# Weight blocks of queries and groups loaded in pairs into a ring of four slots

## The chip, the cores and the metric

The kernel runs on one core of a Trainium2 chip. The metric is the device time of one execution in microseconds (us), the median of several runs. Matrix products run on TensorE (PE), elementwise work on VectorE (DVE), ScalarE (ACT) and GpSimd (POOL); SyncE (SP) issues most transfers between memory and the on-chip buffers. Each engine has a queue of its own, worked through in order; engines wait for each other by semaphores.

## The reference

One layer of a hybrid encoder over 16 meta tokens and 1024 frames of width 2048, all float32, cut to what matters:

```
h    = concat([meta, x])                       # (16 + 1024, 2048)
proj = rmsnorm(h, norm_g) @ w_in               # 2048 -> 4352 columns
pv, pg, q, k, v, ag = split(proj)              # 1024,1024,1024,128,128,1024
pool_out = (trailing_mean(pv, 2|4|8|16) - pv) @ pool_w * pool_scale   # 4 groups of 256
attn_out = softmax([q k^T / 8, sink]) v        # 16 heads of 64, window of 2 chunks of 64 + meta
h = h + concat([silu(pg) * pool_out, silu(ag) * attn_out]) @ w_out
return h[16:]
```

## The kernel before

**Precision by splitting.** Every float32 operand of a big product is split in two fp32r parts. For a block of weights, ACT copies `raw` to `wh` (the high part, `split_high`, line 618), DVE subtracts to get `wl` (the low part, `split_low`, line 966), and PE makes three products: high times high, high times low, low times high (lines 1435, 1436 and 1442).

**Blocks.** The input projection is cut in blocks of 128x512 float32, 256 KB each, laid out by the host in the order of use (`w_in_blocks`). Frames are done in two halves of 512; each half goes through the same 136 blocks: 8 for keys and values, 32 for queries (8 tiles of 4 blocks), and 4 groups of 24 (attention gate, pooled values, pooling gate). In this text blocks are numbered 0 to 271 over both halves in the order of use; in the second half, block 136 + n is block n of the half. The number of a block in its group is called its slot in the program. After them come 112 blocks of the output product, numbered from 272, which the change does not touch.

**Two rings of four.** `raw` has four slots (`RAW = 4`), and so have `wh` and `wl` (`SPLIT = 4`); block n has slot n % 4 in all. The life of block n is:

1. SP waits until block n - 4 has been split by DVE, since that frees the slot of `raw` (`s_wl`, line 399), and issues the load (line 400). Each slot has its own semaphore of landing, `s_raw[slot]`.
2. ACT waits for the landing (line 621) and until PE has finished block n - 4 (`s_blk`, line 624), since that frees the slot of `wh`; then it copies. In ACT's program the split of block n stands three blocks ahead of the products that use it (`LEAD = 3`), among the rest of ACT's work: exponentials, copies of transposed probabilities, tanh of the gates.
3. DVE waits for `wh` and writes `wl` (line 970).
4. PE waits for `wl` and makes the block's 12 or more products; the last one raises `s_blk`.

**The other queues that matter.** In a group, four units of attention are woven between the blocks: PE makes scores, DVE and ACT the softmax, PE transposes the probabilities (line 1605), ACT and DVE split the result (`pt`, `pm`; `p_high`, line 849, and `p_low`, line 1183), and PE multiplies by the values (line 1617). The blocks in the program of each engine at which these stand are fixed by `UNIT_AT`. POOL, beside the sums of pooling, issues 32 transfers of 1 MB (two at each of 16 places) that prepare sums of output weights in memory (`weight_sums`, lines 540 to 558): two places lie in the queries of each half and six at the ends of its first three groups. In the first half's groups 1 to 3, SP also stores finished tiles to memory (`spill`, line 411) after block 6 of the group, and loads frames of the next half (`next_frames`, line 418) after block 14.

Of the kernel before, what the change touches and what calls it, by code (L numbers as in the profile page):

```python
# [21 lines left out]
HALVES = SEQ // HALF  # L22
# [18 lines left out]
ONE = 1  # L41

BLK = 512
TILE_BLKS = 4
RAW = 4
SPLIT = 4
LEAD = 3
KV_BLKS = 2 * TILE_BLKS
Q_BLKS = PAIRS * TILE_BLKS
G_BLKS = 6 * TILE_BLKS  # L50
IN_BLKS = KV_BLKS + Q_BLKS + GROUPS * G_BLKS
# [20 lines left out]
OUT_AT = HALVES * IN_BLKS  # L72
# [18 lines left out]
def hymba_layer(nc, xcat, norm_g, w_in, w_out, pool_w, vecs, consts, out):  # L91
# [6 lines left out]
    with ctx:  # L98
        def sb(name, shape, dt=f32):
            return ctx.enter_context(nc.sbuf_tensor(name, shape, dt))  # L100

        def sem(name):
            return ctx.enter_context(nc.semaphore(name))
# [5 lines left out]
        raw = sb("raw", [P, RAW, BLK])  # L109
# [135 lines left out]
        s_xc = sem("s_xc")  # L245
        s_sp = sem("s_sp")
        s_raw = [sem(f"s_raw{i}") for i in range(RAW)]
        s_pw = sem("s_pw")
        s_init = sem("s_init")
        s_gq = sem("s_gq")  # L250
# [3 lines left out]
        s_wl = sem("s_wl")  # L254
# [140 lines left out]
        def _(sp):  # L395
            def load_block(n, slot, src, free=True):

                if free:
                    sp.wait_ge(s_wl, ONE + n - RAW + 1)
                sp.dma_start(raw[:, slot, :], src).then_inc(s_raw[slot], 16)  # L400

            def first_frames(i):
                k0, k1 = FIRST_LOADS[i]
                lo, hi = k0 % 4 * P, (k1 - 1) % 4 * P + P
                sp.dma_start(mixed[:, k0 // 4:KT:4, lo:hi],
                             xcat[META:META + HALF, k0 * P:k1 * P].rearrange("(r p) c -> p r c", p=P)).then_inc(s_xf[i], 16)
# [4 lines left out]
            def spill(q):  # L411

                sp.wait_ge(s_me, ONE + 2 * (q + 1))
                sp.wait_ge(s_oe, ONE + UNITS * (q + 1))
                for t in (2 * q, HK + 2 * q):
                    sp.dma_start(mx0[t:t + 2, :, :].rearrange("k p c -> p k c"), mixed[:, t:t + 2, :]).then_inc(s_sp, 16)

            def next_frames(q):

                sp.wait_ge(s_sp, 32 * (q + 1))  # L420
                if q:
                    sp.wait_ge(s_xc, 32 * q)
                for i in range(2):
                    t, f = HK * i + 2 * q, META + HALF + 2 * P * i
                    sp.dma_start(mixed[:, t:t + 2, :],
                                 xcat[f:f + 2 * P, q * BLK:(q + 1) * BLK].rearrange("(r p) c -> p r c", p=P)).then_inc(s_xc, 16)

            sp.dma_start(cst[:, 0:P], consts[:, 0:P]).then_inc(s_id, 16)
            sp.dma_start(x_meta, xcat[0:META, :]).then_inc(s_xmeta, 16)
            first_frames(0)  # L430
            first_frames(1)
            first_block(1, free=False)
            first_frames(2)
            first_block(2, free=False)
            first_block(3, free=False)
# [4 lines left out]
            for h in range(HALVES):  # L440
                h0 = h * IN_BLKS
                for n in range(RAW if h == 0 else 0, KV_BLKS):
                    if h and n == KV_BLKS - 1:
                        spill(GROUPS - 1)
                    load_block(h0 + n, n % RAW, w_in[TILE_BLKS * (n % 2) + n // 2, :, :])
                if h:
                    next_frames(GROUPS - 1)
                with sp.Fori(0, PAIRS) as j:
                    for b in range(TILE_BLKS):
                        n = KV_BLKS + j * TILE_BLKS + b  # L450
                        load_block(h0 + n, b % RAW, w_in[n, :, :])

                def group(g):
                    sp.wait_ge(s_pwl, ONE + h * GROUPS + g)
                    sp.dma_start(pw_raw.rearrange("p (a c) -> p a c", a=2),
                                 pool_w[g, :, :].rearrange("(a p) c -> p a c", p=P)).then_inc(s_pw, 16)
                    for b in range(G_BLKS):
                        n = KV_BLKS + Q_BLKS + g * G_BLKS + b
                        load_block(h0 + n, b % RAW, w_in[n, :, :])
                        if h == 0 and g and b == 6:  # L460
                            spill(g - 1)
                        if h == 0 and g and b == 14:
                            next_frames(g - 1)

                if h == 0:
                    for g in range(GROUPS):
                        group(g)
                else:
                    with sp.Fori(0, GROUPS) as g:
                        group(g)  # L470
# [5 lines left out]
            for n in range(OUT_BLKS):  # L476
                p, s = divmod(n, PASS)
# [6 lines left out]
                src = {P1: w_out[top, one], P2: w_out[bottom, one], Q3: w_out[bottom, two]}.get(j)  # L484
                load_block(OUT_AT + n, n % RAW, wsum[kind, p, top, :] if src is None else src)

                if p == 0 and s in A1_AT:
                    i = A1_AT.index(s)
# [125 lines left out]
        def _(act):  # L614
            def copy(dst, src):
                return nc.scalar.activation(dst, src, ACT.Copy)  # L616

            def split_high(n4, off):

                slot = off % RAW  # L620
                act.wait_ge(s_raw[slot], 16 * (n4 + off // RAW + 1))
                if not (isinstance(n4, int) and n4 == 0 and off < SPLIT):

                    act.wait_ge(s_blk, ONE + n4 * RAW + (off - SPLIT + 1))
                copy(wh[:, slot, :], raw[:, slot, :]).then_inc(s_wh, 1)
# [31 lines left out]
            nc.scalar.activation(junk[:, 0:1], kT[:, 0:1], ACT.Sqrt).then_inc(s_table, 1)  # L657
            act.wait_ge(s_table, 1)
            split_high(0, 0)


# [4 lines left out]
            for h in range(HALVES):  # L666
                h4 = h * IN_BLKS // RAW

                for k in range(2 * h, KT):
                    x_high(h, k)  # L670
                    for off in FIRST_SPLITS[h].get(k, ()):
                        split_high(h4, off)
                    for r in FIRST_STATS.get(k, ()) if h == 0 else ():
                        if r == 0:
                            act.wait_ge(s_cst, 16)
                            for i in range(len(FIRST_LOADS)):
                                act.wait_ge(s_xf[i], 16)
                        first_stats(0, r)
                    if h and k in (5, 7, 9, 11):
                        next_stats(2, (k - 5) // 2)  # L680
                    elif h and k >= 14:
                        next_stats(3, k - 14)
# [7 lines left out]
                for s in range(5, KV_BLKS):  # L690
                    split_high(h4, s + LEAD)
                    if s < 7:
                        if h == 0:
                            first_stats(h, s - 3)
                        else:
                            next_stats(3, s - 3)
# [255 lines left out]
            for n in range(OUT_BLKS):  # L952
                p, s = divmod(n, PASS)
# [832 lines left out]
```

## Time and profile before

| | |
|---|---|
| median of 3 runs | 1179.48 us (1178.87 to 1179.82) |
| the profiled execution's own time | 1178.72 us |
| its span, first to last instruction | 1176.6 us |
| PE busy | 1166.1 us |
| DVE busy | 889.7 us |
| ACT busy | 616.1 us |
| weight loads of 256 KB from `w_in_blocks` | 272, 2.7 us from issue to landing in the median |

The profiled execution is one run; its span leaves out 2.1 us that its device time holds before and after. Busy time of an engine is time in which it worked on an instruction. An engine below 100% is either ahead of others and waiting for them, or is waited for; which of the two, only the waits tell.

### The profile page before, as it was taken

The numbers are of one execution on the slowest core, as the hardware profiler recorded it, in microseconds if no ns is written. First come the engines' busy times: TensorE is split into PE (matmuls) and PEld (weight loads), VectorE is DVE, ScalarE is ACT, GpSimd is POOL, SyncE is SP. The second block draws the span as 40 slices with busy tenths as digits, with TensorE's granted clock in tenths as the row PEclk, the third lists the DMA queues.
The fourth block names the chain that finished last, engine by engine and source line by source line (L and its number), as shares of the span: only waits on it lengthen the run. The fifth ranks groups of instructions, "written<-read, shape, count | busy, mean of one in ns | idle before, by whom it ended". The sixth has DMA issues, their size and how long they took to land.

```text
span 1176.6 us, 17280 instructions
## 1 busy us (share of the span) xinstructions
PE 1166.1 (99%) x5882; PEld 991.8 (84%) x5882; DVE 889.7 (76%) x1545; ACT 616.1 (52%) x1400; POOL 115.5 (10%) x133
## 2 busy tenths in 40 slices
PE   7999999999999999999999999999999999999998
PEld 7888898898898988888888888888888888888887
DVE  4678778787786885678788786987977977656676
ACT  5743366554665655643565655655544544444442
POOL 0000011020040220000011030220400000100001
PEclk9999999999999999999999999999999999999999
DMA  7354339455486333445357372392346544553443
GB/s 242 92 162 156 95 99 218 132 189 184 132 177 179 118 90 108 134 138 171 94 129 179 92 242 76 97 226 81 88 137 223 167 136 134 185 176 123 142 145 134
DMA packets 85486, 171.26 MB, mean 146 GB/s; under 512 B 8464, under 2 KB 11792, under 8 KB 85264
## 3 DMA queue, kind: packets, MB, share of 16 engines
q1 hardware_dynamic: 72000, 129.08, 35.3%
q0 software_dynamic: 13120, 40.90, 14.1%
q8 instruction: 44, 0.72, 0.3%
q14 instruction: 34, 0.28, 0.1%
q10 hardware_dynamic: 288, 0.28, 0.1%
HBM read 157.64 MB, written 46.14 MB: 173 GB/s over the span
## 4 chain that ended last, share of the span: by engine, by line
PE 99%; DMA 0%; DVE 0%; ACT 0%; issue 0%; SPq 0%; DVEq 0%; ACTq 0%
PE R L1435 18%; PE R L1436 18%; PE R L1442 18%; PE R L1725 3%; PE R L1723 3%; PE R L1724 3%; PE OP L1725 2%; PE S L1725 2%; PE OP L1723 2%; PE S L1723 2%; PE OP L1724 2%; PE S L1724 2%; PE S L1593 1%; PE OP L1617 1%; PE OP L1442 1%; PE OP L1435 1%
## 5 line engine op out<-in xcount | busy, mean ns | idle before, releaser
L964 DVE TENSOR_TENSOR wl<-raw,wh 128x512 fp32r<-128x512 f32 x384 | 283.4, 740 | 192.9 <-ACT wh L616 190.6
L616 ACT ACTIVATE wh<-raw 128x512 fp32r<-128x512 f32 x384 | 240.8, 629 | 351.0 <-PE OP L1725 165.9
L1435 PE MATMUL R<-act_h,wh 128*128 128x512 f32 (+5 forms) x1056 | 380.6, 365 | 0.0
L1436 PE MATMUL R<-act_l,wh 128*128 128x512 f32 (+5 forms) x1056 | 378.5, 364 | 0.0
L1442 PE MATMUL R<-act_h,wl 128*128 128x512 f32 (+5 forms) x1048 | 362.2, 365 | 0.0
L1436 PEld LDWEIGHTS R<-act_l,wh 128*128 128x128 f32 x1056 | 198.6, 188 | 28.6
L1435 PEld LDWEIGHTS R<-act_h,wh 128*128 128x128 f32 x1056 | 198.3, 188 | 28.7
L1442 PEld LDWEIGHTS R<-act_h,wl 128*128 128x128 f32 x1048 | 188.3, 188 | 32.1
L1725 PE MATMUL R<-wh,mix_l 128*128 128x512 f32 x168 | 65.4, 389 | 0.0
L1723 PE MATMUL R<-wh,mix_h 128*128 128x512 f32 x168 | 65.4, 389 | 0.0
L1724 PE MATMUL R<-wl,mix_h 128*128 128x512 f32 x168 | 65.4, 389 | 0.0
L870 ACT ACTIVATE row_buf<-scr 128x512 f32<-128x512 f32 x32 | 20.2, 632 | 79.5 <-DVE scr L1212 79.5
L1154 DVE TENSOR_REDUCE scr<-S 128x288 f32<-128x576 f32 x56 | 42.3, 756 | 25.3 <-PE S L1593 24.5
L1084 DVE RECIPROCAL scr<-scr 128x512 f32<-128x512 f32 x16 | 53.6, 3347 | 0.0
L844 ACT ACTIVATE scr<-scr,nmax 128x144 f32<-128x144 f32 x128 | 51.2, 403 | 3.4 <-DVE nmax L1162 3.3
L586 POOL TENSOR_TENSOR scr<-scr 128x513 f32<-128x513 f32 (+6 forms) x40 | 50.3, 1257 | 3.1
L578 POOL TENSOR_TENSOR scr<-scr,row_buf 128x512 f32<-128x512 f32 (+4 forms) x16 | 20.9, 1306 | 268.3 <-ACT scr L616 257.9
L1725 PE MATMUL OP<-wh,mix_l 128*128 128x512 f32 x112 | 43.6, 389 | 0.0
L1724 PE MATMUL OP<-wl,mix_h 128*128 128x512 f32 x112 | 43.6, 389 | 0.0
L1723 PE MATMUL S<-wh,mix_h 128*128 128x512 f32 x112 | 43.6, 389 | 0.0
L1724 PE MATMUL S<-wl,mix_h 128*128 128x512 f32 x112 | 43.6, 389 | 0.0
L1725 PE MATMUL S<-wh,mix_l 128*128 128x512 f32 x112 | 43.6, 389 | 0.0
(252 smaller groups left out, 1957.8 us busy)
## 6 DMA issues: line engine op xcount, KB each, us to landing
raw<-w_in_blocks SPq DMA_DIRECT2D x271, 256.0 KB, 2.7
wsum<-w_out_in POOLq DMA_DIRECT2D x24, 1024.0 KB, 12.1
raw<-wsum SPq DMA_DIRECT2D x64, 256.0 KB, 2.6
raw<-w_out_in SPq DMA_DIRECT2D x48, 256.0 KB, 3.3
c<-xcat SPq DMA_DIRECT2D x32, 256.0 KB, 3.5
out<-c POOLq DMA_DIRECT2D x28, 256.0 KB, 2.9
mixed<-xcat SPq DMA_DIRECT2D x10, 512.0 KB, 5.2
mx<-mixed SPq DMA_DIRECT2D x8, 512.0 KB, 3.5
```

Of the source, the lines that this page charges most:

```text
L586: ins = pool.tensor_tensor(dst[:, lo:COLS], src[:, lo:COLS], src[:, lo - step:COLS - step], ALU.add)
L616: return nc.scalar.activation(dst, src, ACT.Copy)
L844: nc.scalar.activation(prob[:, c, :], prob[:, c, :], ACT.Exp, bias=nmax[:, c:c + 1], accum_out=den[:, c:c + 1]).then_inc(s_ex, 1)
L964: return nc.vector.tensor_tensor(dst, a, b, ALU.subtract)
L1084: nc.vector.reciprocal(q_rs[t % 2], q_rs[t % 2]).then_inc(s_qrs, 1)
L1154: nc.vector.tensor_reduce(to, both, AX.X, ALU.add).then_inc(s_sm, 1)
L1435: mm(o, wh[:, b, w], xh, start=(k == 0), stop=False)
L1436: mm(o, wh[:, b, w], xl, start=False, stop=False)
L1442: last = mm(o, wl[:, b, w], xh, start=False, stop=(k == KT - 1))
L1723: mm(banks[r], mh, wh[:, slot, :], start=(k == 0), stop=False)
L1724: mm(banks[r], mh, wl[:, slot, :], start=False, stop=False)
L1725: last = mm(banks[r], ml, wh[:, slot, :], start=False, stop=(k == HK - 1))
```

## The change

The 256 blocks of queries and groups (128 of each half) are loaded two at a time. A pair (n, n + 1) with n even goes with one transfer of 512 KB into two neighbouring slots of `raw`. The number of slots, the splits on ACT and DVE and the products on PE stay as they are. SP now waits before the pair until block n - 3, which held the slot of the second block, has been split; before, block n was loaded as soon as block n - 4 had been split. Each pair of slots has one semaphore of landing, `s_pair`, so ACT's wait for block n ends only when both blocks are there. `landed` gives the semaphore and the count for each block. Keys, values and the output product are still loaded by `load_block`.

```
+        s_pair = [sem(f"s_pair{i}") for i in range(RAW // 2)]
...
+            def load_pair(n, slot, src):
+
+                sp.wait_ge(s_wl, ONE + n + 1 - RAW + 1)
+                sp.dma_start(raw[:, slot:slot + 2, :], src.rearrange("n p c -> p n c")).then_inc(s_pair[slot // 2], 16)
...
-                    for b in range(TILE_BLKS):
+                    for b in range(0, TILE_BLKS, 2):
                         n = KV_BLKS + j * TILE_BLKS + b
-                        load_block(h0 + n, b % RAW, w_in[n, :, :])
+                        load_pair(h0 + n, b % RAW, w_in[bass.ds(n, 2), :, :])
...
-                    for b in range(G_BLKS):
+                    for b in range(0, G_BLKS, 2):
                         n = KV_BLKS + Q_BLKS + g * G_BLKS + b
-                        load_block(h0 + n, b % RAW, w_in[n, :, :])
+                        load_pair(h0 + n, b % RAW, w_in[bass.ds(n, 2), :, :])
                         if h == 0 and g and b == 6:
                             spill(g - 1)
                         if h == 0 and g and b == 14:
...
+            def landed(n):
+
+                kv, rest = KV_BLKS // RAW, (IN_BLKS - KV_BLKS) // RAW
+                if n >= OUT_AT:
+                    return s_raw[n % RAW], 16 * (HALVES * kv + (n - OUT_AT) // RAW + 1)
+                half, b = divmod(n, IN_BLKS)
+                if b < KV_BLKS:
+                    return s_raw[n % RAW], 16 * (half * kv + b // RAW + 1)
+                return s_pair[n % RAW // 2], 16 * (half * rest + (b - KV_BLKS) // RAW + 1)
...
-                act.wait_ge(s_raw[slot], 16 * (n4 + off // RAW + 1))
+                act.wait_ge(*landed(n4 * RAW + off))
```

SP's queue in group 1 of the first half, before (a row is one kind of transfer, with the shape it writes and how many follow each other):

```order
L455 DMA scr<-pool_w_in 128x2x256
L400 DMA raw<-w_in_blocks 128x512 x7
L416 DMA mx<-mixed 128x2x512 x2
L400 DMA raw<-w_in_blocks 128x512 x8
L425 DMA mixed<-xcat 128x2x512 x2
L400 DMA raw<-w_in_blocks 128x512 x9
```

The same group of SP's queue now:

```order
L461 DMA scr<-pool_w_in 128x2x256
L406 DMA raw<-w_in_blocks 128x2x512 x4
L422 DMA mx<-mixed 128x2x512 x2
L406 DMA raw<-w_in_blocks 128x2x512 x4
L431 DMA mixed<-xcat 128x2x512 x2
L406 DMA raw<-w_in_blocks 128x2x512 x4
```

24 loads became 12 of twice the size; the stores of `spill` now stand behind the loads of 8 blocks instead of 7, and the loads of frames behind 16 instead of 15.

## Rows read from the trace of the kernel before

**Rows 1.** The page, parts 1, 2 and 4: busy time, granted clock, ending chain.

```profile
span 1176.6 us, 17280 instructions
...
PE 1166.1 (99%) x5882; PEld 991.8 (84%) x5882; DVE 889.7 (76%) x1545; ACT 616.1 (52%) x1400; POOL 115.5 (10%) x133
...
PEclk9999999999999999999999999999999999999999
...
PE 99%; DMA 0%; DVE 0%; ACT 0%; issue 0%; SPq 0%; DVEq 0%; ACTq 0%
```

**Rows 2.** Waits of PE (total us, times, longest us), and busy time by stretch.

```profile
PE R L1453 <- DMA scr<-xcat: 5.7, 1, 5.7
PE R L1495 <- DVE act_l L976: 1.0, 1, 1.0
PE OP L1495 <- DVE act_l L976: 0.2, 1, 0.2
...
480.00:866.00 386.00, 386.00 (x1815) 322.17 (x1814) 309.54 (x554) 210.67 (x517) 48.13 (x44) 1.00 0.49 133
```

**Rows 3.** Waits ahead of ACT's split of weights, by what ended them.

```profile
ACT wh L616 <- PE OP L1725: 165.9, 108, 2.4
ACT wh L616 <- PE R L1442: 160.7, 126, 2.8
...
ACT wh L616 <- DMA raw<-w_in_blocks: 9.2, 5, 3.4
```

**Rows 4.** Transfers by source: count, KB each, median us to landing.

```profile
raw<-w_in_blocks SPq DMA_DIRECT2D x271, 256.0 KB, 2.7
wsum<-w_out_in POOLq DMA_DIRECT2D x24, 1024.0 KB, 12.1
...
mixed<-xcat SPq DMA_DIRECT2D x10, 512.0 KB, 5.2
mx<-mixed SPq DMA_DIRECT2D x8, 512.0 KB, 3.5
```

**Rows 5.** Timeline, quiet: DVE splits block 95, the next load, block 98 on ACT, DVE, PE.

```profile
301.44 0.69 DVE L964 TENSOR_TENSOR wl<-raw,wh 128x512 fp32r<-128x512 f32 x1 [1.61 <-ACT wh L616]
302.16 0.33 SPq L400 DMA_DIRECT2D raw<-w_in_blocks  x1
309.76 0.63 ACT L616 ACTIVATE wh<-raw 128x512 fp32r<-128x512 f32 x1 [0.63 <-PE R L1442]
311.85 0.68 DVE L964 TENSOR_TENSOR wl<-raw,wh 128x512 fp32r<-128x512 f32 x1
318.94 0.28 PE L1435 MATMUL R<-act_h,wh 128*128 128x264 f32 x1
```

**Rows 6.** Timeline: blocks 143 and 146 at the start of the second half.

```profile
468.96 0.68 DVE L964 TENSOR_TENSOR wl<-raw,wh 128x512 fp32r<-128x512 f32 x1
472.05 0.62 ACT L616 ACTIVATE wh<-raw 128x512 fp32r<-128x512 f32 x1
476.02 0.29 ACT L715 ACTIVATE scr<-xsd 128x128 f32<-128x128 f32 x1
478.10 0.27 PE L1528 MATMUL PT<-cst,scr 128*128 128x128 f32 x1
```

**Rows 7.** Timeline: one of POOL's 16 places, at the end of group 2 (first half).

```profile
344.27 2.06 POOL L556 DMA_DIRECT2D wsum<-w_out_in  x2
```

**Rows 8.** The load of block 109, its time to landing, ACT's splits of 108 and 109.

```profile
333.96 0.33 SPq L400 DMA_DIRECT2D raw<-w_in_blocks  x1
DMA to landing us min/median/max: 8.5/8.5/8.5
342.16 0.62 ACT L616 ACTIVATE wh<-raw 128x512 fp32r<-128x512 f32 x1
344.88 0.63 ACT L616 ACTIVATE wh<-raw 128x512 fp32r<-128x512 f32 x1 [2.10 <-PE R L1442]
```

**Rows 9.** Loads of blocks 112 and 113; ACT, DVE and PE behind block 112.

```profile
344.91 0.33 SPq L400 DMA_DIRECT2D raw<-w_in_blocks  x1
DMA to landing us min/median/max: 8.4/8.4/8.4
346.43 0.33 SPq L400 DMA_DIRECT2D raw<-w_in_blocks  x1
DMA to landing us min/median/max: 9.1/9.1/9.1
354.25 0.62 ACT L616 ACTIVATE wh<-raw 128x512 fp32r<-128x512 f32 x1
356.55 1.19 DVE L964 TENSOR_TENSOR pm<-OP,pm 16x128 fp32r<-16x128 f32 x4 [0.34 <-ACT pm L616]
359.56 0.64 PE L1617 MATMUL OP<-pt,v_s 128*128 128x256 f32 x4
```

**Rows 10.** The same in the second half: block 249's load, then the chain behind 248.

```profile
773.35 0.33 SPq L400 DMA_DIRECT2D raw<-w_in_blocks  x1
DMA to landing us min/median/max: 9.4/9.4/9.4
781.47 0.61 ACT L616 ACTIVATE wh<-raw 128x512 fp32r<-128x512 f32 x1
783.77 1.19 DVE L964 TENSOR_TENSOR pm<-OP,pm 16x128 fp32r<-16x128 f32 x4 [0.33 <-ACT pm L616]
786.50 0.64 PE L1617 MATMUL OP<-pt,v_s 128*128 128x256 f32 x4
```

**Rows 11.** Second half, group 0: block 197's load, the chain behind block 196.

```profile
610.16 0.33 SPq L400 DMA_DIRECT2D raw<-w_in_blocks  x1
DMA to landing us min/median/max: 7.4/7.4/7.4
617.17 0.63 ACT L616 ACTIVATE wh<-raw 128x512 fp32r<-128x512 f32 x1
620.72 0.63 ACT L616 ACTIVATE wh<-raw 128x512 fp32r<-128x512 f32 x1 [0.74 <-PE R L1442]
629.06 0.22 DVE L1179 TENSOR_TENSOR pnm<-scr,rden 128x64 f32<-128x64 f32 x1
629.37 0.62 PE L1605 MATMUL PT<-cst,scr 128*128 128x128 f32 x4
```

## The prediction

> **What bounds the kernel now.** I read the page first. TensorE is busy for 1166.1 us of a span of 1176.6 us, its granted clock is full in all 40 slices, and the chain that ended last is TensorE for 99% [rows 1]. So a change can win only what TensorE idles, 10.5 us at most, and it loses whatever idle time it puts into TensorE. Next the waits of TensorE: only three are listed, 5.7, 1.0 and 0.2 us, for the meta tokens' transfer at the very start and for DVE's split of the frames, and none for a weight block. From 480 to 866 us, which is nearly all the part of the second half that the change touches, it is busy for 386.00 of 386.00 us [rows 2]. Last, who waits for loads: ACT's split of weights waits hundreds of microseconds for TensorE to free a slot (165.9 and 160.7 us are the two largest) and only 9.2 us, five times, for a load [rows 3]. Loads run ahead of ACT, ACT ahead of TensorE. There is nothing for a better load to win on the path that sets the end.
>
> **What the change removes.** 128 issues of about 0.33 us on SP and 128 landings. SP issues and then waits for DVE's splits; nobody waits for SP's own 0.33 us. That is worth 0. In the groups of the first half the stores of finished tiles and the loads of frames each slip behind one more block: about one block time, some 3 us, and the frames are wanted a group later. Worth 0.
>
> A 256 KB load takes 2.7 us in the median [rows 4]. The Trainium skill would promise more of larger ones: its page "DMA: Bandwidth & Descriptors", section "Anatomy of one DMA", gives a fixed cost of about 2.0 us a transfer and 436 GB/s beyond it, that is 2.6 us for 256 KB (the trace agrees) and, as an estimate, 3.2 us for 512 KB; its section "Bandwidth" advises batches of 1 MB or more. By that rule 128 fixed costs go away, 256 us of transfer latency in all, and by the trace none of it is on the path.
>
> **What it adds: the even block comes later.** The pair (n, n + 1) is issued when block n + 1 used to be, since both wait until block n - 3 is split. So block n + 1 keeps its issue time, and block n is issued later by what lay between the two. And ACT needs block n first, with both now landing together. The question is how far ahead of ACT the odd block's landing lies. I compared these times for all 128 even blocks; two kinds of stretch differ.
>
> *Quiet stretches.* What a 512 KB load to the chip takes is not in the trace, only two other kinds of 512 KB transfer: 3.5 us for stores of tiles and 5.2 us for loads of frames, which run partly under other traffic [rows 4]. I take 3.5, nearest to the undisturbed 2.7 of half the size, and keep 5.2 for the range. A typical place: block 95 is split by DVE at 302.13 (301.44 + 0.69), the pair (98, 99) is issued at 302.16 and lands at 305.7; ACT splits block 98 at 309.76, 4.1 us later [rows 5]. Over all 128 places the median margin is 3.2 us, in the queries mostly 2 to 3. One quiet place fails, at the second half's start: block 143 is split at 469.64, the pair (146, 147) lands at 469.8 + 3.5 = 473.2, and ACT wants it at 472.05, so ACT is late by 1.1 us. Behind it ACT makes the columns that TensorE transposes; they are done at 476.31 and TensorE takes them at 478.10, a cover of 1.8 us [rows 6]. Cost 0; with 5.2 us, late by 2.8, cost 1.0.
>
> *Contended stretches.* At 16 places POOL issues two transfers of 1 MB, as at 344.27 [rows 7]; they take 12.1 us in the median [rows 4], and beside them a weight load takes 6 to 9 us. Here the pair can't land before the odd block did. It lands later still by what the even block's 256 KB take, if these were through before: in this stretch the landings of queued loads follow each other by about 2.1 us (blocks 112 and 113: 344.91 + 8.4 = 353.3 and 346.43 + 9.1 = 355.5, 2.2 apart [rows 9]). Bounds: 0 and 2.1 us on top of the odd block's landing. I take 0.8, since in most of these pairs the even block was itself still queued when the odd one was issued, so that its bytes are counted already. With 0 on top 14 of the 128 even blocks make ACT wait, 10 us in sum; with 0.8, 23 blocks, 23 us; at the far bounds (2.1, and 5.2 us in quiet) 36 blocks, 62 us. Against the 9.2 us of load waits now [rows 3], ACT's waits for loads should come out at some 25 to 35 us.
>
> **What of that reaches TensorE.** A weight split has its own cover: it stands three blocks ahead of its products. Block 98's `wl` is done at 312.53 and its first product starts at 318.94, a cover of 6.4 us [rows 5]; over all 256 blocks of the change the median is 6.8, and only blocks 8 and 144, which are not late, have less than 3.2. That covers the latenesses above by itself. What is thin is the attention work that stands behind a late split in ACT's queue. The late places, by what follows them:
> - Blocks 108, 110, 244 and their like (fourth-last and second-last of a group, and the whole of the queries): late by 0.3 to 2.9. For 108: the odd block lands at 333.96 + 8.5 = 342.5, ACT wants block 108 at 342.16, late 0.3 to 2.4; but ACT then idles 2.10 us waiting for TensorE before block 109 [rows 8]. Absorbed: 0 (at the far bound some 0.3 to 0.8 each).
> - Block 112: late by 355.5 - 354.25 = 1.2 at least, 2.0 by my value, 3.3 at most. Behind it ACT copies `pt` and `pm`, DVE finishes `pm` at 357.74, and TensorE's value products start at 359.56: a cover of 1.8 us [rows 9]. Cost 0 / 0.2 / 1.5.
> - Block 248: the odd block lands at 773.35 + 9.4 = 782.8, ACT wants 781.47: late 1.3 / 2.1 / 3.4; `pm` is done at 784.96, and the products start at 786.50, a cover of 1.5 [rows 10]. Cost 0 / 0.6 / 1.9. Block 224 is like it, late 0.4 / 1.2 / 2.5 with 1.8 of cover: 0 / 0 / 0.7.
> - Block 196: the odd one lands at 610.16 + 7.4 = 617.6, wanted at 617.17: late 0.4 / 1.2 / 2.5. ACT idles 0.74 us three microseconds later, yet the unit's probabilities are done at 629.28 and their transposes start at 629.37, a cover of only 0.1 us at the end of DVE's queue [rows 11]. Between them DVE has short waits of its own, so I take 0 / 0.3 / 1.0.
> - All others (60, 66, 114, 200, 220 and so on): late by 0 / 0 to 1.0 / up to 2.3 with covers above 1.3: 0 / 0 / 1.0 in sum.
>
> Sum at my values: 0.2 + 0.6 + 0.3 = 1.1 us of new idle time on TensorE. Lowest 0; at the far bounds 1.5 + 1.9 + 0.7 + 1.0 + 1.0 + 1.0 (block 146) = 7.1 us. The instructions of TensorE stay the same, and its clock has no reason to fall with idle times of a microsecond.
>
> The profiled execution took 1178.72 us; with 1.1 it is 1179.8. The median of the runs shown, 1179.48, lies 0.76 above it, so I forecast 1180.6. What this measurement can tell from no change is about 0.2%, 2.4 us: below 1177.1 faster, above 1181.8 slower.
>
> **The rivals.**
> 1. *The ring of four is in effect a ring of two, and ACT's lateness gets through.* The mechanism is one: under POOL's traffic a pair lands 2 us behind the old odd block, ACT's split is late by 2 to 3.4 us, and the copy of probabilities behind it starves the value products at 112, 224, 248 and 196. For it: the 2.2 us between queued landings, and that a stall in the first pair delays DVE's split and with it the next pair. Against: ACT's idle time behind every second late split, and the covers of 1.5 to 1.8. Its price is the far sum, 4 to 7 us: 1183 to 1187. It decides from about 2 us of extra landing time on. This is the rival on the slower side.
> 2. *Nothing reaches TensorE.* The pair lands when the odd block did, every lateness is 1.3 us or less and all is covered: 1179.5. For it: the bytes in the queues are the same. Against: only little; it differs from my forecast by 1.1 us and falls in the same class.
> 3. *It becomes faster,* since fewer transfers leave more room for POOL's sums and for the first loads. TensorE has 6.9 us of waits [rows 2], all before the first pair or for frames; a shorter queue could give back perhaps 0.2 us of them. To be 2.4 us faster, TensorE's own instructions would have to run faster beside fewer transfers, for which no row speaks.
> 4. *The change does not do what it says,* that is the 512 KB transfer is carried out as two loads in a row and takes twice as long, 5.4 us, everywhere. Then 5.2 above is the quiet figure: 0 to 2 us on top, 1181.5.
>
> **How the numbers follow.** My forecast, 0.5 to 2.3 us slower, 0.40; rival 2, 0.30; rival 1, 0.22; rival 4, 0.05, half of it over the bound; rival 3, 0.03. Faster 0.03; slower 0.22 + 0.02 = 0.24; the same 0.73. The range reaches from 1178.8, what the median itself scatters on the low side, to 1184.5, which holds the lower part of rival 1.
>
> **What would show it.** In the changed profile: 128 transfers of 512 KB with a median landing time near 3.5 us (well above 4.5 speaks for rival 4); ACT's waits for these loads of 20 to 35 us in some 20 places, most of them beside POOL's 1 MB transfers; TensorE's waits still short, with the new ones, if any, ahead of the value products (now line 1633) near 360 and 786 us or the transposes near 629 us; weight products (now line 1451) waiting for `wl` nowhere. If TensorE waits for `wl` itself, or its new waits add up to over 2.4 us, I am wrong on the cover; if the span shrinks by more than 2 us, I am wrong on the bound.

## The result, and the profile after

The changed kernel takes 1190.42 us in the median of 4 runs (1190.13 to 1191.1), the one before 1179.65 beside it: 10.8 us slower, a ratio of 1.009 with a 95% interval of 1.0078 to 1.0102. The forecast was 1180.6 with a range up to 1184.5. The profiled execution's own time is 1190.54 us, its span 1188.4 us.

The page's parts 1 and 6 after the change answer to [rows 1] and [rows 4]:

```profile
span 1188.4 us, 16928 instructions
...
PE 1170.3 (98%) x5882; PEld 993.6 (84%) x5882; DVE 888.1 (75%) x1545; ACT 617.1 (52%) x1400; POOL 115.5 (10%) x133
...
raw<-w_in_blocks SPq DMA_DIRECT2D x128, 512.0 KB, 3.7
wsum<-w_out_in POOLq DMA_DIRECT2D x24, 1024.0 KB, 12.2
```

The waits of TensorE after the change, all of them (total us, times, longest us), against [rows 2]; and ACT's waits for loads, against [rows 3]:

```profile
PE R L1469 <- DMA scr<-xcat: 5.4, 1, 5.4
PE PT L1621 <- DVE pnm L1195: 2.0, 2, 1.1
PE OP L1633 <- ACT pm L622: 1.9, 2, 1.1
PE OP L1633 <- DVE pm L980: 1.9, 1, 1.9
PE OP L1574 <- DVE d_l L980: 1.7, 1, 1.7
PE R L1511 <- DVE act_l L992: 1.0, 1, 1.0
PE OP L1633 <- issue: 0.5, 1, 0.5
PE OP L1511 <- DVE act_l L992: 0.2, 1, 0.2
```

```profile
ACT wh L622 <- DMA raw<-w_in_blocks: 33.7, 17, 5.7
```

TensorE has five new kinds of wait, 8.0 us in sum, in seven places, and none is for a weight block. They stand ahead of the transposes of probabilities (L1621), the value products (L1633) and the sums of squares of the queries (L1574). ACT's waits for loads went from 9.2 to 33.7 us.

Where the time went, by the ends of the blocks on TensorE, before against after. Each step is the growth of the difference at one block:

| block at which TensorE falls behind | time in the changed profile, us | step, us |
|---|---|---|
| start to block 32, small steps both ways | up to 118 | 0.5 |
| 33 (queries, first half) | 121 | 2.0 |
| 61 and 63 (end of group 0, first half) | 207, 214 | 1.9 |
| 111 (end of group 2, first half) | 369 | 1.3 |
| 195, 197, 199 (end of group 0, second half) | 633 to 647 | 2.6 |
| 247 (end of group 2, second half) | 802 | 3.7 |
| sum, with small steps between | | 11.8 |

The sum is the growth of the span in the two profiled executions. Between these places nothing is lost. The three other executions of the changed kernel have spans of 1187.1 to 1187.2 us, over 1 us shorter than the profiled one, and the medians differ by 10.8, so not every execution has all of the 11.8 us.

**The place at block 34,** which the prediction had priced at 0. Before, with the times of ACT, DVE and TensorE there:

```profile
110.15 0.63 ACT L616 ACTIVATE wh<-raw 128x512 fp32r<-128x512 f32 x1 [2.09 <-PE R L1442]
...
112.81 0.60 ACT L773 ACTIVATE scr<-R 128x512 f32<-128x512 f32 x1 [1.08 <-PE R L1442]
113.31 0.59 ACT L773 ACTIVATE d_h<-R 128x512 fp32r<-128x512 f32 x1
...
114.48 0.69 DVE L964 TENSOR_TENSOR d_l<-scr,d_h 128x512 fp32r<-128x512 f32 x1
...
115.11 0.39 PE L1442 MATMUL OP<-act_h,wl 128*128 128x512 f32 x1
115.33 0.40 PE L1558 MATMUL OP<-d_h,pw_h 128*128 128x512 f32 x1
```

and after, with the pair's issue and its time to landing in front:

```profile
105.01 0.37 SPq L406 DMA_DIRECT2D raw<-w_in_blocks  x1
...
DMA to landing us min/median/max: 9.2/9.2/9.2
...
114.22 0.63 ACT L622 ACTIVATE wh<-raw 128x512 fp32r<-128x512 f32 x1 [5.68 <-DMA raw<-w_in_blocks]
...
116.32 0.59 ACT L789 ACTIVATE d_h<-R 128x512 fp32r<-128x512 f32 x1
...
116.94 0.69 DVE L980 TENSOR_TENSOR d_l<-scr,d_h 128x512 fp32r<-128x512 f32 x1 [0.36 <-ACT d_h L789]
...
117.69 0.50 PE L1574 MATMUL OP<-d_h,pw_h 128*128 128x512 f32 x1 [1.72 <-DVE d_l L980]
```

The pair lands at 105.01 + 9.2 = 114.2 and ends ACT's idle time of 5.68 us. Before, ACT idled 2.09 us there, for TensorE; so the load makes it 3.6 us late. Behind block 34 in ACT's queue stand the squares of a query tile (`d_h`). The cover on this chain was 1.08 us of idle time on ACT ahead of the squares, 0.58 us between their high part (done at 113.90) and DVE's start on the low part (114.48), and 0.16 us between DVE's end (114.48 + 0.69 = 115.17) and TensorE's start (115.33): 1.8 us in all. The other 1.8 us reach TensorE, which waits 1.72 us.

**The place at block 248,** which answers to [rows 10]. The columns of the last two rows are the stretch, its length, the busy us of PE, PEld, DVE, ACT and POOL with their instructions, the granted clock as a share of full speed, the DMA share and GB/s:

```profile
782.89 0.37 SPq L406 DMA_DIRECT2D raw<-w_in_blocks  x1
...
DMA to landing us min/median/max: 10.2/10.2/10.2
...
793.08 0.63 ACT L622 ACTIVATE wh<-raw 128x512 fp32r<-128x512 f32 x1 [2.46 <-DMA raw<-w_in_blocks]
...
795.39 1.19 DVE L980 TENSOR_TENSOR pm<-OP,pm 16x128 fp32r<-16x128 f32 x4 [0.34 <-ACT pm L622]
...
796.63 0.94 PE L1633 MATMUL OP<-pt,v_s 128*128 128x256 f32 x4 [1.86 <-DVE pm L980]
...
797.00:800.40 3.40, 3.40 (x13) 2.81 (x12) 2.81 (x6) 2.55 (x6) 0.00 (x0) 0.50 0.65 128
800.40:806.00 5.60, 5.60 (x26) 4.59 (x25) 4.77 (x10) 1.16 (x2) 0.00 (x0) 1.00 0.16 60
```

The chain is the one of [rows 10], moved: landing, ACT's split, the copies of `pm`, value products, and the cover of 1.5 us is used up. Then comes what no term held: after the 1.86 us of idle time TensorE runs for 3.4 us at the lower granted clock (1.2 instead of 2.4 GHz), which costs 1.7 us more and explains why this step is 3.7 and not 2. It does not come each time: in the profiles of experiments 3 and 9 this place idles 1.46 and 1.82 us and the clock stays full.

The pair of block 248 was not only slow to land, it was also issued late. It waits for DVE's split of block 245, which in turn came late because block 244 did. Before, the split of block 245, and after, ACT and DVE behind the landing of the pair (244, 245) at 779.8 (the profile puts ACT's wait down to TensorE, but it ends with this landing; so it is missing in the 33.7 us):

```profile
772.48 0.69 DVE L964 TENSOR_TENSOR wl<-raw,wh 128x512 fp32r<-128x512 f32 x1
...
779.84 1.15 ACT L622 ACTIVATE wh<-raw 128x512 fp32r<-128x512 f32 x2 [2.47 <-PE R L1458]
...
780.50 0.69 DVE L980 TENSOR_TENSOR wl<-raw,wh 128x512 fp32r<-128x512 f32 x1 [1.96 <-ACT wh L622]
...
782.02 0.69 DVE L980 TENSOR_TENSOR wl<-raw,wh 128x512 fp32r<-128x512 f32 x1
```

The split of block 245 moved by 9.5 us (772.48 to 782.02) where TensorE was only 8.1 us behind, so the pair of block 248 (issued at 782.89) went 1.4 us late. The same happens to the second late pair at the other ends of groups: 0.7 us at block 112, 1.2 us at 64 and at 200.

### The profile page after: what moved, and what is told of

It reads as the page before. It is cut to its first block, busy times and chain, and to the rows that moved or that the text cites. A ratio compares the mean times of both kernels' runs of the same rounds, so it can differ in the third digit from the quotient of the medians.

```text
span 1188.4 us, 16928 instructions
## 1 busy us (share of the span) xinstructions
PE 1170.3 (98%) x5882; PEld 993.6 (84%) x5882; DVE 888.1 (75%) x1545; ACT 617.1 (52%) x1400; POOL 115.5 (10%) x133
## 4 chain that ended last, share of the span: by engine, by line
PE 88%; DMA 6%; DVE 3%; ACT 1%; issue 1%; SPq 0%; ACTq 0%; DVEq 0%
PE R L1451 15%; PE R L1452 15%; PE R L1458 15%; DMA raw<-w_in_blocks 6%; PE R L1739 3%; PE R L1741 3%; PE R L1740 3%; PE S L1739 2%; PE OP L1739 2%; PE OP L1741 2%; PE S L1741 2%; PE OP L1740 2%; PE S L1740 2%; PE S L1609 1%; PE OP L1458 1%; PE OP L1452 1%
## 5 line engine op out<-in xcount | busy, mean ns | idle before, releaser
L1739 PE MATMUL OP<-wh,mix_h 128*128 128x512 f32 x112 | 43.6, 389 | 0.0
```

The source lines that it names most:

```text
L1739: mm(banks[r], mh, wh[:, slot, :], start=(k == 0), stop=False)
```

## The experiments

Each was timed in runs beside the kernel before; "over before" is the difference of the two medians.

**1. Two singles issued when the pair was issued,** each with its own semaphore (change against the kernel before):

```
-                    sp.wait_ge(s_wl, ONE + n - RAW + 1)
+                    sp.wait_ge(s_wl, ONE + n + ahead - RAW + 1)
...
-                        load_block(h0 + n, b % RAW, w_in[n, :, :])
+                        load_block(h0 + n, b % RAW, w_in[n, :, :], free=b % 2 == 0, ahead=1)
```

> Two single loads of 256 KB, each with its own semaphore, both issued when the pair was issued (the even block waits until block n - 3 is split). Nothing else differs from the kernel before. Theory A, the late issue costs: nearly the whole loss of 10.8 us stays, 8 to 11 us, with ACT waiting 25 us or more for loads. Theory B, the common landing costs (ACT needs the even block and gets it only with the odd one): beside POOL's transfers the even block lands 1 to 2 us ahead of the odd one, every lateness shrinks by that, and the loss falls to 0 to 4 us. My guess is 4 us, a part from each.

Measured: 1181.59 us, 1.8 over before, ratio 1.0015 (1.0005 to 1.0024). Its ACT waits 16.8 us for loads, and TensorE has one new wait of 0.8 us before the sums of squares and two short ones before the value products. With a semaphore for each block, the late issue costs about a sixth of the loss. At block 248, the loads of both blocks and then ACT:

```profile
775.90 0.33 SPq L400 DMA_DIRECT2D raw<-w_in_blocks  x1
DMA to landing us min/median/max: 9.0/9.0/9.0
776.43 0.33 SPq L400 DMA_DIRECT2D raw<-w_in_blocks  x1
DMA to landing us min/median/max: 10.6/10.6/10.6
...
784.93 0.63 ACT L616 ACTIVATE wh<-raw 128x512 fp32r<-128x512 f32 x1 [0.95 <-DMA raw<-w_in_blocks]
...
788.90 0.64 PE L1617 MATMUL OP<-pt,v_s 128*128 128x256 f32 x4
```

Block 248 lands at 784.9 and 249 at 787.0, and ACT goes on with the first. Its wait is 0.95 us instead of 2.46, and the value products wait for nothing.

**9. The same two singles, but with the pair's one semaphore** (against the changed kernel; the count per pair is 32 in `landed`):

```
-                sp.dma_start(raw[:, slot:slot + 2, :], src.rearrange("n p c -> p n c")).then_inc(s_pair[slot // 2], 16)
+                for i in range(2):
+                    sp.dma_start(raw[:, slot + i, :], src[i]).then_inc(s_pair[slot // 2], 16)
...
```

> As the changed kernel, but each pair goes as two transfers of 256 KB issued one behind the other, both raising the pair's one semaphore, so that ACT still gets the even block only with the odd one. Against the run with two semaphores (1.8 us over before) only the common landing differs. Theory B, the common landing costs: 9 us or more over before, since the odd single landed about 1 us later than the pair of 512 KB beside POOL's traffic; 1189 to 1194. Theory C, one transfer of 512 KB is itself the slow thing: 1181 to 1182.

Measured: 1192.41 us, 13.1 over before, ratio 1.0112 (1.0094 to 1.013). Nothing but the semaphore differs from experiment 1, and 11 us lie between them: theory B, as far as these two go (experiment 10 bounds it). At block 248, the two loads, ACT and TensorE:

```profile
784.04 0.33 SPq L407 DMA_DIRECT2D raw<-w_in_blocks  x1
DMA to landing us min/median/max: 7.5/7.5/7.5
784.57 0.33 SPq L407 DMA_DIRECT2D raw<-w_in_blocks  x1
DMA to landing us min/median/max: 9.1/9.1/9.1
...
793.69 0.63 ACT L623 ACTIVATE wh<-raw 128x512 fp32r<-128x512 f32 x1 [2.60 <-DMA raw<-w_in_blocks]
...
797.24 0.75 PE L1634 MATMUL OP<-pt,v_s 128*128 128x256 f32 x4 [1.82 <-DVE pm L981]
```

Block 248 is there at 791.5, but ACT may start only when 249 is, at 793.7. Here TensorE idles 1.82 us and the clock stays full, and the step is 2.1 us. The size of the transfer is not what costs: over the 34 pairs whose odd block took over 4 us to land before, the pair of the changed kernel landed 7.1 us after its issue in the mean, and the second of the two singles 7.2 us after the first one's issue here and 8.1 us in experiment 1.

**2 and 3. Pairs in the queries only, pairs in the groups only.** The other part is loaded by `load_block` as before, and `landed` counts accordingly:

```
+PAIRED = range(KV_BLKS, KV_BLKS + Q_BLKS)              # experiment 2
+PAIRED = range(KV_BLKS + Q_BLKS, IN_BLKS)              # experiment 3
```

> Pairs in the queries only, groups as before. If the stalls of TensorE belong to places, only the one seen at 118 us of the changed profile (2.0 us, in the queries) stays: 1181 to 1182.5, with a new wait of TensorE of about 1.7 us before the sums of squares. Rival, the pairs cost something everywhere (issue, more time of each load): a quarter of the loss, 2.7 us, spread over many blocks.

> Pairs in the groups only, queries as before. By the places of the stalls in the changed profile (1.9 near block 60, 1.3 at 111, 2.5 near 196, 3.7 at 247) the loss is 9 to 9.5 us: 1188.5 to 1189.5. If the stalls were chained (each moves the next), the sum of this run's and of the queries' loss would differ from 10.8 by over 2 us.

Measured: 1182.34 us (2.6 over; ratio 1.0025, 1.0016 to 1.0035) and 1188.34 us (8.6 over; 1.0075, 1.0058 to 1.0091), in sum 11.2 against 10.8, well within the intervals: no sign that one place's stall moves the other's. (The profile of experiment 3 lacks the slow clock at 797 us, and its execution is the fastest of the four.) The one new wait of TensorE with pairs in the queries alone is the one at block 33:

```profile
PE OP L1576 <- DVE d_l L982: 1.9, 1, 1.9
```

**4. Pairs only away from POOL's traffic,** 82 of the 128:

```
+PAIRED = [b for b in range(KV_BLKS, KV_BLKS + Q_BLKS, 2) if b not in (20, 22, 24, 34, 36)]
+PAIRED += [KV_BLKS + Q_BLKS + g * G_BLKS + b for g in range(GROUPS) for b in range(0, G_BLKS, 2)
+           if not (g < GROUPS - 1 and b >= 20) and not (g and b < 8)]
```

> Pairs for 82 of the 128, all but those whose loads run beside POOL's transfers of 1 MB (blocks 20 to 25, 34 to 37 of a half; the last four blocks of groups 0 to 2 and the first eight of groups 1 to 3), which are loaded singly as before; SP's loops are written out. If the loss is all from lateness under that traffic, the time is that of before within 1 us, ACT's waits for loads stay under 14 us, and TensorE has no new wait. If pairs cost by themselves, about two thirds of the loss stay, 7 us.

Measured: 1179.82 us, 0.1 over before, ratio 1.0 (0.999 to 1.001). ACT waits 11.3 us for loads, TensorE has no new wait. So pairs away from POOL's traffic cost nothing; they also win nothing.

**5 and 6. POOL's transfers cut from 512 rows to 8 rows,** in the changed kernel and in the one before. The sums of output weights are left out, and the output product reads the weights themselves:

```
-                load_block(OUT_AT + n, n % RAW, wsum[kind, p, top, :] if src is None else src)
+                load_block(OUT_AT + n, n % RAW, w_out[top, one] if src is None else src)
...
-                    rows = slice(i * HALF, (i + 1) * HALF)
+                    rows = slice(i * HALF, i * HALF + 8)
...
```

> The changed kernel with POOL's 32 transfers cut from 512 rows to 8 rows each (same count, same semaphores); the output product's weights that came from these sums are read from the output weights instead, so the sums of weights are left out. If the late pairs come from that traffic, pairs land 3.6 us after issue everywhere, only block 146 makes ACT wait (about 1.3 us), TensorE gets no new wait, and the time is within 1.5 us of the kernel before with the same cut. If the late issue alone costs, most of the 10.8 us stays between the two.

> The kernel before with the same cut of POOL's transfers, as a base for the run beside it; the sums of weights are left out. Nothing of it was on TensorE's path, so 1179 to 1180 us, ACT waiting for loads under 4 us.

Measured: 1180.53 and 1179.6 us; against the same runs of the kernel before the ratios are 1.0008 (0.9998 to 1.0018) and 0.9998 (0.9989 to 1.0008). Without the traffic the change costs 0.9 us, which ten runs of each hardly tell from nothing, and the spans of the two profiles are 1176.6 and 1176.5. So the traffic is needed for the loss. ACT waits four times, 4.0 us, for loads; two of these are at single blocks at the very start, and two, 1.3 and 1.1 us, are for the pairs at blocks 146 and 150, of which only the first was expected:

```profile
ACT wh L622 <- DMA raw<-w_in_blocks: 4.0, 4, 1.3
```

**7 and 8. The copies of all probabilities ahead of the weight split,** in both kernels:

```
-                        todo[at[u] + 6].append((p_high, u))
+                        first[at[u] + 6] = [(p_high, u)]
...
+                        for f, *a in first.get(s, ()):
+                            f(*a)
                         if s < G_BLKS:
                             split_high(n4, s + LEAD)
...
-                        todo[at[u] + 6].append((p_low, u))
+                        ahead[at[u] + 6].insert(0, (p_low, u))
```

> The changed kernel with one change in the programs of ACT and DVE: in each slot of a group the copies of the probabilities (p_high on ACT, p_low on DVE) stand ahead of the weight split instead of behind it. If a late weight split costs only because the attention work queues behind it, the stalls ahead of the value products go (about 4.4 us of TensorE's waits) and the loss falls to 3 to 6 us, with ACT's waits for loads still near 34 us. If TensorE waits for the weights themselves, nothing is won.

> The kernel before with the same move of p_high and p_low ahead of the weight split, as a base. No load is late here, so within 1 us of before; a split that now waits for TensorE's transposes could cost up to 2 us.

Measured: 1205.74 and 1198.84 us. The kernel that was to be the base is itself 19 us slower: DVE now takes up the sums of scores later, and TensorE waits for them 21 times, 14 us in sum. Between the two lie 6.9 us instead of 10.8, which points the way expected, but on so disturbed a base it shows nothing.

**11 and 12. The same move for the last unit of a group only** (slot 21, where no scores follow):

```
-                        todo[at[u] + 6].append((p_high, u))
+                        (first if u == UNITS - 1 else todo).setdefault(at[u] + 6, []).append((p_high, u))
...
-                        todo[at[u] + 6].append((p_low, u))
+                        (ahead if u == UNITS - 1 else todo)[at[u] + 6].append((p_low, u))
```

> The changed kernel with p_high and p_low ahead of the weight split for the last unit of a group only (slot 21), where no score follows on DVE. Theory: a late split of block 112 or 248 costs because the last unit's probabilities stand behind it. Then the stalls near 366 us (1.3) and 797 us (1.9, and 1.7 of slow clock behind it) go, and those at 120, 205 and 636 stay: 1185 to 1187. If TensorE waits there for another reason, the time stays at 1190.

> The kernel before with the same move in slot 21 only, as a base: the split there waits up to 0.8 us longer for the transposes, which nothing feels: 1179 to 1181. When all four units were moved, the base lost 19 us, through scores that DVE took up later.

Measured: 1184.92 us (5.6 over before; ratio 1.0046, 1.0032 to 1.0059) and 1180.38 us (1.0008, 0.9998 to 1.0017). The base stays within 0.8 us of before, and half of the loss is gone, as expected. What TensorE waits for in experiment 11 beyond the first three waits of before:

```profile
PE OP L1577 <- DVE d_l L983: 2.3, 1, 2.3
PE PT L1624 <- DVE pnm L1198: 1.7, 2, 1.4
```

No value product waits any more, though ACT's waits for loads are as long as ever (35.4 us). So at the ends of the groups it was not the weights that came too late for the value products, but the probabilities queued behind them on ACT. The stalls in the queries and ahead of the transposes, which this move does not touch, stay.

**10. Three slots of four,** every single load issued one block later (against the kernel before; `ahead` as in experiment 1):

```
-                        load_block(h0 + n, b % RAW, w_in[n, :, :])
+                        load_block(h0 + n, b % RAW, w_in[n, :, :], ahead=1)
```

> Single loads as before, but each block of queries and groups, even or odd, waits until block n - 3 is split, so that only three of the four slots of raw are in use. Even blocks are as late as with two semaphores; odd blocks, until now 2 to 8 us ahead of ACT, are issued about 3 us later too. If what counts is ACT's margin beside POOL's traffic, odd blocks stay mostly in time, and the loss is 2 to 6 us, at the same places. If it is the common landing alone that matters, under 2 us.

Measured: 1204.43 us, 25.1 over before, ratio 1.0204 (1.0182 to 1.0225), four times the upper end I had given. ACT now waits 28 times, 50.9 us, and 14 of these waits are at odd blocks, where I had expected few; those at blocks 21, 157 and 169 in the queries stop TensorE for 2.7 to 3.5 us each through the sums of squares. Theory B in its strict form, only the common landing matters, fails here: what counts is when a block is there against when ACT comes to it, whatever makes it late.

## Why the prediction was wrong

- **What bounds the kernel** was right: TensorE, with no wait for weight blocks, so nothing to win. Experiment 4 wins nothing.
- **What the change adds** was right in kind. The pair is issued when the odd block was, and lands in 3.7 us in quiet stretches (3.5 forecast; the 3.2 estimated beside it was too low). ACT waits 33.7 us in 17 places (25 to 35 in some 20 forecast). Block 146 makes ACT wait and TensorE not, as said. So the sum of ACT's lateness was right; how it was spread, and what of it passed through, was not.
- **The step that failed first is "I take 0.8":** one value for what the pair's landing adds to the odd block's, at every place beside POOL's transfers. Over the 34 such pairs it added 0.4 us in the mean, but from -2.3 to 3.0. At block 34 it was 2.3 (9.2 us from issue to landing against 6.9), at 60 3.0, at 196 and 246 2.3, beyond my bound of 2.1 each time. A stall begins only where the cover ends, so the few large values cost and the many small ones give nothing back. My reason, that the even block's bytes were queued already and so counted, held in the mean but not there: at these four places the even block had been in the queue, and still the pair came 2.3 to 3.0 us later than the odd block had. Why the landing scatters so is open.
- **The step that failed second is "So block n + 1 keeps its issue time".** It holds for the first late pair at the end of a group, not for the next one, since DVE's split of block n - 3 is late itself. At block 248 the landing added only 0.7 us, less than my 0.8; the other 1.4 us came from the late issue. Rival 1 names this chain ("a stall in the first pair delays DVE's split"), but my sum left it out. What came together, as lateness of ACT in us, rounded:

| block | odd block's landing behind ACT, before | later issue, TensorE's own delay taken out | added by the landing | late | I had taken |
|---|---|---|---|---|---|
| 34 | 1.3 | 0 | 2.3 | 3.6 | in the queries, absorbed |
| 60 | -0.6 | 0 | 3.0 | 2.4 | 0 to 1.0 |
| 112 | 1.3 | 0.7 | 1.0 | 2.9 | 2.0 |
| 196 | 0.4 | 0 | 2.3 | 2.7 | 1.2 |
| 248 | 1.3 | 1.4 | 0.7 | 3.5 | 2.1 |

- **The step that failed third is "and the whole of the queries ... Absorbed: 0".** I had looked for idle time of ACT behind the late split, but the chain behind block 34 had 1.8 us of cover, less than the 3.6 us by which the split was late, and less than the 3.4 us that its 1.3 us and my far bound of 2.1 make. 2.0 us were lost there, and experiment 2 shows it alone (2.6 in the median). The cover of the chain behind each late block had to be read for the queries too, as it was for the groups.
- **Group 0** (blocks 60 to 64 and 196 to 200) was priced at 0.3 us with a far bound of 2.0; it cost 1.9 + 2.6 us. ACT waited for a load twice in each end of the group, and the unit's transposes and its value products both stalled. I had counted block 60 among those "with covers above 1.3"; the transposes behind it had 0.2 us (199.96 to 200.15), no more than the 0.1 us behind block 196:

```profile
199.74 0.22 DVE L1179 TENSOR_TENSOR pnm<-scr,rden 128x64 f32<-128x64 f32 x1
...
200.15 0.60 PE L1605 MATMUL PT<-cst,scr 128*128 128x128 f32 x4
```

- **Blocks 112 and 248:** 1.3 and about 2.0 us against my 0.2 and 0.6, at the far bounds (1.5 and 1.9), and the slow clock on top, 1.7 us more. I had excluded it by "its clock has no reason to fall with idle times of a microsecond"; the idle time was 1.86.
- **The rivals.** Rival 1, the slower one, is the nearest to what happened: the late copies of probabilities starve the value products at 112 and 248 and in group 0, though not at 224, which cost nothing. Its price of 4 to 7 us lacked the queries and the clock. Experiments 1 and 9 add what it did not name: the even block must wait for the odd one's bytes. Rival 4 is out by the 3.7 us.
- In the profile's terms: 8.0 us of new waits, 1.7 of half clock, 0.5 before block 33, in sum 10.2 of 11.8. The remaining 1.6 us lie in the same seven places. In the profile TensorE's products overlap: at block 34 each is recorded for 0.39 us, but the next starts after 0.22 (115.11 and 115.33). A stall loses that overlap, and the first product behind it is drawn out (0.50 us instead of 0.40), so the starts there moved by 1.97 us for a wait of 1.72. Read from the starts, the seven stalls make 9.7 us instead of 8.0.

## What to carry to other kernels

When transfers into a ring are merged, the first block is issued only when the last one may be, and usable only when the last one has landed. So ask not how long the larger transfer takes, but how long before its reader the last block used to land. And do not price a scattered latency by one value: a cover takes in the small delays, and only the large ones cost. Read the margin where transfers of other queues run, not in the median; here the 82 pairs away from traffic cost nothing and the other 46 cost it all. An engine that waits for one late input delays what stands behind it in its queue: the cover to read is that of the work behind, and putting that work first gave back half of the loss.

## What the runs showed of the hardware

- Beside POOL's transfers of 1 MB, loads on SP's queue take much longer than alone, and it is not their size: 256 KB took mostly 6 to 9 us there in the kernel before (2.7 in the median of all), and 512 KB up to 10.4 us in the changed one. With that traffic cut (experiment 5), 512 KB land in 3.5 to 4.3 us at all 34 of these places.
- TensorE's clock fell to half for 3.4 us after an idle time of 1.86 us (changed kernel, 797 us), but not after 1.82 us at the same place in experiment 9, nor after 1.88 to 2.35 us at five others (experiments 2, 7, 9, 10 and 11), nor after 2.67 us at 525 us in experiment 10. In experiment 10 it fell for 3.4 us around idle times of 2.79 and 3.05 us, and for 6.8 us around one of 3.48. The stretch of the three slots kernel at 562 us, with the wait that ends there:

```profile
562.46 0.80 PE L1558 MATMUL OP<-d_h,pw_h 128*128 128x512 f32 x1 [2.79 <-DVE d_l L964]
...
562.50:566.00 3.50, 3.50 (x10) 2.83 (x11) 2.62 (x5) 0.63 (x1) 0.00 (x0) 0.59 0.60 199
```

  So in these profiles one of eight idle times between 1.8 and 2.7 us cost another 1.7 us, and the three longer ones in mid-kernel 1.7 to 3.4 us each.
